# A one-core attention and expert layer: projections in another order, index scores and modulation sums beside a projection, suffix sums as fp32r products

## What is computed

```python
mod = silu(c) @ w_ada + b_ada            # six rows of 1024: shift1, scale1, gate1, shift2, scale2, gate2
h = rmsnorm(x, norm1_g) * (1 + scale1) + shift1
q_a,k_a,v_a, q_b,k_b,v_b, q_i,k_i,w_i, g_a,g_b = split(h @ w_in)   # four projections are 512 wide
# branch A, stick-breaking attention, 8 heads, strictly causal
z = q_a @ k_a.T * dh**-0.5
log_1m = where(before, log_sigmoid(-z), 0)
a = where(before, exp(log_sigmoid(z) + suffix_sum_of_later_keys(log_1m)), 0)
o_a = a @ v_a
# branch B: an indexer picks 128 keys for each query, then softmax attention with a position bias
score = sum_h w_i * relu(q_i @ k_i.T);  sel = top_k(score, 128)
o_b = softmax(rmsnorm(q_b) @ rmsnorm(k_b)[sel].T * dh**-0.5 + bias) @ v_b[sel]
x = x + gate1 * ((sigmoid(g_a)*(o_a @ w_o_a) + sigmoid(g_b)*(o_b @ w_o_b)) @ w_out)
# then a mixture of 16 experts, which the change leaves alone
```

## Time and profile before

| | |
|---|---|
| median of 3 runs | 805.81 us (804.68 to 807.87) |
| the profiled execution | 804.75 us, its span 802.8 us |
| PE busy | 747.3 us, 93% of the span |
| DVE busy | 615.5 us, 77% |
| ACT busy | 429.9 us, 54% |
| granted PE clock, mean | 0.988 |

### The profile page before, as it was taken

One profiled execution on the slowest core, in us unless ns is written; L12 is line 12 of the kernel. 1 busy time (PEld: TensorE's weight loads), 2 busy tenths in 40 slices (PEclk: granted clock), 3 DMA queues, 4 the chain that ended last, 5 costly groups with the idle time before them and its releaser, 6 DMA issues.

```text
span 802.8 us, 9975 instructions
## 1 busy us (share of the span) xinstructions
PE 747.3 (93%) x3617; PEld 569.3 (71%) x3619; DVE 615.5 (77%) x805; ACT 429.9 (54%) x516; POOL 109.2 (14%) x91
## 2 busy tenths in 40 slices
PE   3899999999999898999999988999999999999992
PEld 3777687776665555667888864788888887888782
DVE  5876886533999958653567657899999999999991
ACT  5433215357575443556423433776677777676760
POOL 4110000000010000002000011013233132413111
PEclk9999999999999999999999999999999999999997
DMA  9929996110130131105438246999999999999983
GB/s 268 353 79 383 386 362 229 52 53 1 53 106 1 55 103 53 53 7 196 138 116 298 111 176 209 415 399 373 385 387 386 387 387 386 387 385 381 372 289 56
DMA packets 87307, 184.93 MB, mean 230 GB/s; under 512 B 8112, under 2 KB 27672, under 8 KB 85216
## 3 DMA queue, kind: packets, MB, share of 16 engines
q1 hardware_dynamic: 79200, 156.29, 51.9%
q0 software_dynamic: 8064, 28.09, 12.2%
HBM read 171.74 MB, written 12.62 MB: 230 GB/s over the span
## 4 chain that ended last, share of the span: by engine, by line
PE 50%; DVE 28%; issue 7%; DMA 7%; ACT 5%; DVEq 1%; POOL 0%; SPq 0%; ACTq 0%; POOLq 0%
PE ps L666 13%; PE ps L668 12%; PE ps L667 12%; DVE w_lo L1963 8%; DMA raw<-in_w_gate 3%; DVE score L1783 3%; DVE m L1782 2%; DVE ys L2083 2%; ACT w_hi L1506 2%; DMA raw<-in_w_in 2%; DVE w_lo L1602 2%; PE ps L924 1%; DVE accm L1664 1%; DVE score L1769 1%; PE ps L940 1%
## 5 line engine op out<-in xcount | busy, mean ns | idle before, releaser
L1963 DVE TENSOR_TENSOR w_lo<-raw,w_hi 128x2048 fp32r<-128x2048 f32 x80 | 179.7, 2284 | 5.6 <-ACT w_hi L1506 5.6
L1506 ACT ACTIVATE w_hi<-raw 128x2048 fp32r<-128x2048 f32 x80 | 151.2, 1915 | 11.1 <-DMA raw<-in_w_gate 4.8
L666 PE MATMUL ps<-w_lo,hgT_hi 128*128 128x512 f32 x256 | 103.4, 404 | 4.6 <-DVE hgT_lo L2105 1.5
L666 PE MATMUL ps<-act_lo,w_hi 128*128 128x512 f32 x232 | 98.3, 424 | 5.1 <-DVE act_lo L1647 3.9
L667 PE MATMUL ps<-w_hi,hgT_lo 128*128 128x512 f32 x256 | 100.2, 391 | 0.0
L668 PE MATMUL ps<-w_hi,hgT_hi 128*128 128x512 f32 x256 | 100.0, 391 | 0.0
L668 PE MATMUL ps<-act_hi,w_hi 128*128 128x512 f32 x232 | 91.1, 393 | 0.0
L667 PE MATMUL ps<-act_hi,w_lo 128*128 128x512 f32 x232 | 91.0, 392 | 0.0
L1244 ACT ACTIVATE w_hi<-raw 128x2048 fp32r<-128x2048 f32 (+2 forms) x29 | 52.0, 1796 | 71.9 <-DMA raw<-in_w_in 48.8
L1602 DVE TENSOR_TENSOR w_lo<-raw,w_hi 128x2048 fp32r<-128x2048 f32 (+2 forms) x29 | 61.9, 2144 | 33.0 <-ACT w_hi L1244 32.8
L619 POOL DMA_INDIRECT out<-ys,slot_tok x15 | 48.9, 3257 | 159.9 <-DVE ys L2083 159.9
(11 more groups left out here) (283 smaller groups left out, 1361.8 us busy)
## 6 DMA issues: line engine op xcount, KB each, us to landing
raw<-in_w_down SPq DMA_DIRECT2D x32, 1024.0 KB, 15.7
raw<-in_w_gate SPq DMA_DIRECT2D x30, 1024.0 KB, 17.7
raw<-in_w_up SPq DMA_DIRECT2D x18, 1024.0 KB, 16.2
raw<-in_w_in SPq DMA_DIRECT2D x16, 1024.0 KB, 6.4
raw<-in_w_ada SPq DMA_DIRECT2D x16, 1024.0 KB, 7.2
raw_late<-in_w_up SPq DMA_DIRECT2D x14, 1024.0 KB, 18.2
raw<-in_w_ada SPq DMA_DIRECT2D x8, 512.0 KB, 6.7
raw_early<-in_w_ada SPq DMA_DIRECT2D x8, 512.0 KB, 6.5
```

Source lines behind the costliest of these rows:

```text
L666: pe.matmul(o, a[0], b[1], start=start, stop=False)
L1506: act.activation(e_hi[s_][:, :], e_raw[r][:, :], ACT.Copy).then_inc(e_top, 1)
L1963: dve.tensor_tensor(e_lo[s_][:, :], e_raw[r][:, :], e_hi[s_][:, :].bitcast(F32), ALU.subtract).then_inc(e_split, 1)
```

## The change

The order of the projections becomes qi, ka, qa, va, and that of the chunks qi, qi, 2 ada, ka, 3 ada, ka, 5 ada, qa, 6 ada, qa, va, va. The wait for a PSUM half is made bank by bank. DVE normalises q_b and k_b earlier: the squares after the first chunk of ka, the rest after the second. The transposes of q_b and k_b and the index products of query blocks 1 and 2 (11 tasks, `early_side`) are issued on PE between the half groups of the projection qa (a half group is six products), from the third half group on, in banks 4 to 7, which ka used; the first of them waits for ACT's copies of ka. The two modulation sums follow there as four products of 32 columns of ones each, into four quarters of one bank (`ada_sums`). DVE does the scores of blocks 1 and 2 and all 16 top-k rounds of block 1 before phase A. In phase A the mask is added to the logits right behind z (so line 1736 goes), line 1746's running sums go, ACT makes a float32r copy of the softplus tile (`soft_high`), DVE subtracts it (`soft_low`), and `suffix` multiplies both parts of the tile and of every later key block with the triangle and the matrix of -1 in fp32r. Two top-k rounds per step instead of three or four, none in phase B. Six gate products stand ahead of phase B's first logits.

```diff
+        add_in("qi", C_QI)
+        add_in("ka", C_KA)
         add_in("qa", C_QA)
-        add_in("ka", C_KA)
-        add_in("qi", C_QI)
         add_in("va", C_VA)
...
-        for ch, n in zip(chunks[N_EARLY:], (0, 0, 4, 4, 3, 5, 0, 0)):
+        for ch, n in zip(chunks[N_EARLY:], (0, 0, 2, 3, 5, 6, 0, 0)):
...
-        SEGS = [("misc", 1, None), ("qb", 0, False), ("qa", 1, True), ("ada1", 0, None),
-                ("ka", 1, True), ("ada2", 1, None), ("qi", 0, True), ("va", 1, False)]
+        SEGS = [("misc", 1, None), ("qb", 0, False), ("qi", 0, True), ("ka", 1, True), ("qa", 0, True), ("va", 1, False)]
...
+        N_TURN = 3
+        EARLY_SIDE = [("tr", n, 0) for n in range(N_TURN)] + [("idx", 1 + n // HP, n % HP) for n in range(2 * HP)]
+        SIDE_AT = 2
+        ADA_AT = SIDE_AT + len(EARLY_SIDE)
...
-        FILL_B = [4 * (len(STEPS) - 1) + 4 * (p + 1) for p in range(len(UNITS))]
+        FILL_T = 4 * (len(STEPS) - 1) + 6
+        FILL_B = [FILL_T + 4 * (p + 1) for p in range(len(UNITS))]
...
# PE, seg: bank by bank, and a call after every half group
+                        if ci == 0 and half_before(name):
+                            pe.wait_ge(evac[SEGS[seg_at[name]][1]], half_before(name) - 3 + m)
...
+                            if k == 1 and after:
+                                after(8 * ci + 2 * m)
...
+            def ada_sums(part):
+                pe.wait_ge(chunk_split, first[f"ada{part}"][-1] + 1)
+                pe.wait_ge(early_sb, len(EARLY_SIDE) - 1)
+                for j in range(4):
+                    last = pe.matmul(ps[5 + part][32 * j:32 * j + 32, :], ones[:, 0:32],
+                                     acc[part % 2][:, 512 * j:512 * j + 512], start=True, stop=True)
...
+            def early_side(n):
+                kind, a, hp = EARLY_SIDE[n]
+                b0 = 4 + 2 * (n % 2)
+                if n == 0:
+                    pe.wait_ge(qk_norm, 1)
+                    pe.wait_ge(evac[1], half_before("va"))
+                elif n >= 2:
+                    pe.wait_ge(early_sb, n - 1)
...
+            seg("qi", H)
+            pe.wait_ge(bias_sb, 2)
+            seg("ka", H)
+            seg("qa", H, None, beside_qa)
...
# PE, z and suffix
+                for r in range(2):
+                    last = pe.matmul(zt[m % 2][:, r, 0:P], identb[:, :], neg_ge[:, :], start=False, stop=False,
+                                     skip_group_check=True)
...
+                pe.wait_ge(sp_split, m + 1)
...
+                for j in range(i, NT):
+                    for part in (sp_lo, sp_hi):
+                        for r in range(2):
+                            last = pe.matmul(zt[m % 2][:, r, P * (j - i):S - P * i], neg_r[:, 1 if j > i else 0, :],
+                                             sp_tile(hp, j, part)[:, r, :], start=False,
+                                             stop=(j == NT - 1 and part is sp_hi), skip_group_check=True)
...
# ACT, after the copies of qb
             high(next(todo))
-            act.wait_ge(st_bias, 16)
+            act.wait_ge(qk_var, 1)
+            act.activation(st[:, :, :], st[:, :, :], ACT.Sqrt, bias=epsc[:, 0:1], scale=1.0 / DH).then_inc(qk_sd, 1)
             high(next(todo))
-            seg_copy("qa", qaT, SCALE)
+            seg_copy("qi", qiT)
             high(next(todo))
-            mod_rows(1)
             high(next(todo))
             seg_copy("ka", kaT)
+            for n in range(5):
+                early_side(n)
             high(next(todo))
...
# ACT, step m of phase A
                 gate_rows(FILL_A[m])
+                if m + 1 < len(STEPS):
+                    soft_high(m + 1)
                 weights(m)
...
# DVE
-            raw_chunks(first["va"][0] - N_EARLY - 1)
+            raw_chunks(first["ka"][0] - N_EARLY)
...
+            raw_chunks(first["ka"][1] - first["ka"][0])
             dve.wait_ge(qk_sd, 1)
...
-            raw_chunks(3)
+            raw_chunks(first["qa"][1] - first["ka"][1])
...
+            early_side(0)
+            early_side(1)
+            raw_chunks(1)
+            for q in range(2, 5):
+                early_side(q)
+            raw_chunks(1)
+            for q in range(5, 8):
+                early_side(q)
+            topk_rounds(TOPK // 8)
+            raw_chunks(1)
...
                 gate_splits(FILL_A[m])
-                topk_rounds(2)
-                sums(m)
-                topk_rounds(2 if m < 8 else 1)
+                topk_rounds(1)
+                if m + 1 < len(STEPS):
+                    soft_low(m + 1)
+                topk_rounds(1)
```

More of the change, by code:

```diff
@@ L697, in seg @@
                             last.then_inc(w_used, 1)
[L699 to L707, removed]
+                        if after:
+                            after(8 * ci + 2 * m + 1)
+            def ada_sums(part):
[4 more added lines that the diff above has]
+                                     acc[part % 2][:, 512 * j:512 * j + 512], start=True, stop=True)
+                last.then_inc(ada_ps, 1)
             pe.wait_ge(early_ok, 1)
@@ L857, in av_a, with side_task @@
                 last.then_inc(oa_ps, 1)
[L859 to L877, removed]
+            def side_task(hp):
+                if hp:
+                    pe.wait_ge(side_sb, hp)
+                for r in range(2):
+                    last = pe.matmul(sd[:, r, :], head(qiT, 2 * hp + r, S - P, S), kiT[DH * r:DH * r + DH, :],
+                                     start=True, stop=True, skip_group_check=True)
                 last.then_inc(side_ps, 1)
@@ L904, in _ @@
                     z(m + 1)
-                for t in side_a[m]:
-                    side_task(*t)
+                if 1 <= m <= N_SIDE:
+                    side_task(m - 1)
                 gates_to(FILL_A[m])
@@ L1294, in seg_copy, with mod_row, early_side @@
                     act.activation(dst[:, m, :], bank(name, m)[:, :], ACT.Copy, scale=scale).then_inc(evac[half], 1)
[L1296 to L1303, removed]
+            def mod_row(part):
+                act.wait_ge(ada_ps, part)
+                act.activation(modrow[part - 1][:, :], ps[5 + part][:, :], ACT.Copy).then_inc(ada_sb, 1)
+            def early_side(n):
+                kind, a, hp = EARLY_SIDE[n]
+                act.wait_ge(early_ps, n + 1)
+                b0 = 4 + 2 * (n % 2)
+                if kind == "idx":
+                    q = n - N_TURN
+                    if q >= 2:
+                        act.wait_ge(score_ok, 2 * (q - 1))
+                    act.activation(rel_early[q % 2][:, :, 0:P * (a + 1)], psum[:, b0:b0 + 2, 0:P * (a + 1)], ACT.Relu
+                                   ).then_inc(early_sb, 1)
+                elif a < 2:
+                    act.activation(qbT[:, 2 * a:2 * a + 2, :], psum[:, b0:b0 + 2, :], ACT.Copy, scale=SCALE
+                                   ).then_inc(early_sb, 1)
+                else:
+                    act.activation(kbT[:, :], ps[b0][:, :], ACT.Copy).then_inc(early_sb, 1)
             act.wait_ge(seg_ready, seg_done("misc", 0))
@@ L1363, in soft, with soft_high @@
                 act.activation(t, t, ACT.Ln, bias=1.0).then_inc(z_soft, 1)
+            def soft_high(m):
+                hp, i = STEPS[m]
+                act.wait_ge(sp_ready, m + 1)
+                act.activation(sp_tile(hp, i, sp_hi)[:, :, :], sp_tile(hp, i, sp_x)[:, :, :], ACT.Copy).then_inc(sp_high, 1)
             def weights(m):
@@ L1390, in _ @@
             soft(1)
+            soft_high(0)
             high(next(todo))
@@ L1773, in side_task, with early_side @@
                     rounds.extend((a, r) for r in range(TOPK // 8))
+            def early_side(q):
+                _, a, hp = EARLY_SIDE[N_TURN + q]
+                dve.wait_ge(early_sb, N_TURN + q + 1)
+                score_heads(a, hp, rel_early[q % 2])
+            def side_task(hp):
+                assert all(a != 1 for a, _ in rounds)
+                dve.wait_ge(side_sb, hp + 1)
+                score_heads(3, hp, rel)
             def topk_rounds(count):
@@ L1854, in _ @@
             dve.wait_ge(oa_ps, HP)
+            assert not rounds
             rows(0)
```

192 lines of the change are left out of this document (93 added, 99 removed).

## The result

The changed kernel takes 826.86 us (median of 4 runs, 825.09 to 831.66) against 806.72 for the kernel before in the same comparison (median of 4, 804.68 to 807.87): 1.0263 times as long, interval 1.0231 to 1.0295. Slower, as forecast, but by 20 us and not by 8; 826.9 lies outside 804 to 823. The profiled execution took 828.12 us, its span is 826.3.

What follows compares the result with a forecast made beforehand. PE was taken as the bounding engine, so only its idle time or removed work counts. Projection +18.2, phase A -8.0 and phase B -2 give +8.2 on the profiled 804.75: 813, as a median 814 us, range 804 to 823.

Steps and rivals of the forecast that it cites:

- Projection stage: Before phase A: PE waits 15.2 us for ka's copies at the first early task; phase A begins 18.2 us later.
- rival of dearer products: Quarter modulation sums run one after another (+4.7), narrow fp32r products cost 0.23 not 0.12 (some +3): 822 us; chance 0.17.
- Phase A: Removed mask and running-sum wait against a new softplus loop: 100.5 us instead of 108.55, -8.0.
- bounds of 92 to 105: Phase A's length: 92 if PE alone sets the pace, 105 if DVE's rounds and gate copies enter the loop.
- loop through `soft_high`: Phase A: weights(m) wait behind the next tile's float32r copy; 7.8 us per step for i = 0, 6.3 for i = 1.
- softplus that comes late behind the rounds: Phase A on DVE: without its cover, a softplus behind two rounds is late by up to a round, 1.5 us.
- Phase B: Gains of 4.9 and 1 us against +4 given back: sum -2, bounds 0 to -5.
- Given back: Phase B: gate and weight copies ahead of row sums, last vb product without cover: +4 us, from 0 to 7.
- The two gains named beside it: Phase B: block 3's rounds, idle time and lower clock go, -4.9; gate products fill idle time before the logits, -1.
- That PE alone sets phase A: Rival: PE's list hides the softplus loop in every step; phase A 92 us, total 805.5, no change; chance 0.13.
- ka's wait is short: Rival, first early task: second qa chunk lands earlier, giving 806 us, or 797 if before 116; chance 0.12.

Runs made afterwards that it cites:

- ka_copies_first: Changed kernel with ACT's copies of ka and first five early tasks ahead of the second qa chunk: 816.47 us, 1.0132 times the kernel before.
- two_ada_late_alone: Changed kernel with only the last two ada chunks moved behind the second chunk of qa: 823.4 us, 1.0223 times the kernel before.
- weights_first: Changed kernel with ACT's weights of step m ahead of the float32r copy of step m+1: 819.78 us, 1.0183 times the kernel before.
- gates_as_before: Changed kernel with the six gate products put back behind phase B's first logits: 815.85 us, 1.0144 times the kernel before.
- before_gates_moved: Kernel before with only the six gate products moved ahead of phase B's first logits: 814.31 us, 1.0112 times the kernel before.
- qa_copy_between_tasks: three_and_two_ada_late with ACT's copy of the second qa chunk ahead of the copies of index products 1 and 2: 797.36 us, 0.9885 times the kernel before.
- three_and_two_ada_late: Changed kernel with ka copies first, weights before float32r copy, gates as before, last two ada chunks behind qa's second chunk: 798.13 us, 0.9902 times the kernel before.
- after_again: The changed kernel run once more with no edit: 828.07 us, 1.0267 times the kernel before.

## Why the forecast was right about the direction and wrong about the size

The profiled execution is 23.5 us longer where 8.2 were forecast. Of the 15.3 us between, 7.6 are phase B, 3.7 the start, 2.8 phase A and 1.4 the projection stage. Phase B is the largest, but alone it would have left the forecast at 821.6, just inside its range; the others carry it out.

**Projection stage: right, step by step.** Forecast +18.2, measured +19.6. The first early task was to start 63.5 us into the stage (134.9 less 71.4) and started 63.8 in (138.87 less 75.1); behind it 53.7 were forecast and 54.8 measured. ka_copies_first and two_ada_late_alone show the cause: with the copies moved the wait goes, with the load 4.6 us earlier it shrinks by 4.5. The modulation sums, taken at 1.3 us each, took 1.07, nearer to 0.9 than to 3.67:

```profile
165.25 1.07 PE L711 MATMUL ps<-acc,ones 128*32 128x512 f32 x8
```

The Trainium skill, page TensorEngine Tiling (Array Packing), section Tiling Modes, has four tiles of 32 columns that work independently; this row agrees, as 3.67 / 4 is 0.92. The first half of the rival of dearer products falls with the 1.07.

**Phase A: right in its mechanism, short by a third of its gain.** Forecast -8.0, measured -5.2, inside the bounds of 92 to 105. The loop through `soft_high` sets the wide steps, as weights_first shows (-6.1 without it, with the window's PE busy time unchanged at 93). Steps i = 1 and 0 of the second pair and i = 3 of the third came out at the forecast's 6.3, 7.8 and 6.0 to within 0.1; in the third and fourth pair i = 1 takes 6.8. There the prediction had costed DVE at nothing, "under 90%", though it named a softplus that comes late behind the rounds as the possible price. DVE was busy for only 75.6 of the 103.3 us; it is the order of its list that tells, by the rows, as no run tests it alone: ACT's Ln is done at 255.5, and softplus starts 0.7 later, behind a round of block 3.

```profile
254.68 0.85 ACT L1401 ACTIVATE sp<-sp 128x768 f32<-128x768 f32 x1
```
```profile
255.49 0.68 DVE L1835 MATCH_REPLACE8 score<-m,score 128x512 f32<-128x512 f32 x1
256.20 0.96 DVE L1782 SCALAR_TENSOR_TENSOR sp<-ps,sp 128x768 f32<-128x768 f32 x1
```

z(15)'s chain takes 11.2 instead of 10.8, with 0.46 of wait for `soft_low`. These make half of the 2.8 us missed. The other half are smaller sizes: z(2) starts 2.4 us into the stage and not 1.9; i = 2 takes 6.6 in the third and fourth pair, where 6.4 were taken; and steps i = 3 and 2 of the second pair, where PE also does an index product of block 3 each, take 7.2 and 7.85, 0.65 more than forecast with the 2 us for these products. Without the loop, in weights_first, all these steps of i = 2 and 3 take the same, so the loop doesn't set them. The second half of the rival of dearer products falls: the suffix of i = 0 runs from 241.13 to 243.63, 2.5 us (forecast 2.55).

**Phase B: this step failed.** The prediction put it so: "Given back: the gate blocks now end ahead of a unit's row sums, so that ACT's gate copy and a weight copy of 1.9 stand before them every fourth unit, and the last product with vb has no gates to hide the transposed copies: I put +4, from 0 to 7." The place and the two waits were right; the term was mis-sized. The two gains named beside it came: 96.45 less these 4.9 and 1 is 90.5, and gates_as_before, which has the first but keeps the wait at the logits, measures 92.2. Against 90.5 the 102.0 us of the changed kernel are 11.5 given back, not 4, and above the upper bound of 7. They are 6.0 of the 6.9 us of waits for rows (0.9 at the first unit was there before too: 4.1 in two, of which the earlier trace rows shows 3.19), the 2.9 ahead of the last product, and the lower clock behind the two longest waits, by the windows shown 5.0 x 0.12 + 5.0 x 0.22 + 1.0 x 0.17 + 1.0 x 0.50 = 2.4: together 11.3.

Two links were missing in the sum. ACT doesn't only make the two copies ahead of the Exps, it first waits for the gate block to end, 3 to 7 us a time (`gate_b` waits 37.3 us in eight, 18.4 in the kernel before). And `obT_hi` stands behind the Exps, DVE waits for it with the row sums of the next unit queued behind (38.4 us in eight, 6.5 before). I had priced two copies; what counted was the chain of two engines that begins only when the block ends, against the 5 us that PE has until it needs the rows. That the gates' place alone makes this, gates_as_before and before_gates_moved show from both sides (-10 and +6.9). What each of the two links costs is read from the trace; no run separates them.

**The start.** 3.7 us of the profiled difference were no part of any step; they arise in the first 30 us, and I had no term for a span that starts late. Not all of them came with the lower clock of the last section: ACT's first `hfull` starts at 19.07 instead of 17.78, 1.3 us late, while the granted clock is still 1.00. Without the 3.7 the profiled execution lies 19.7 above that of before.

**The rivals.** That PE alone sets phase A is refuted (5.4 us of waits for weights); that ka's wait is short is refuted (14.12); dearer products are refuted by the rows above. 822 for that rival was the nearest number on record, and right for no reason it gave.

## What to carry to other kernels

When work is moved between two engines that hand each other small pieces, write down at which point of a unit each handed-over piece ends and what its consumer has queued behind it: gate products and their copies that moved from behind a unit's Exps to ahead of them cost 7 us in before_gates_moved with not one instruction added. A blocking wait is priced by what its engine does after it, on this engine and the next, and not by the copy itself: the copies of ka, the weights and the gates were all ready or nearly so, and late for a neighbour in the same list. Three reorderings of a few lines each turn this change from 20 us slower into 9 us faster, so a bad total does not condemn the parts.

## What was not expected of the hardware

The same instructions at the start of the program are granted different clocks in different executions. In the windows from 20 to 30 us the changed kernel had this:

```profile
20.00:22.00 2.00, 0.67 (x3) 1.00 1.04 352
22.00:24.00 2.00, 2.00 (x12) 0.55 1.04 347
24.00:26.00 2.00, 2.00 (x10) 0.50 1.12 359
```

and weights_first, whose program is the same up to phase A, this:

```profile
22.00:24.00 2.00, 2.00 (x16) 1.00 1.00 337
24.00:26.00 2.00, 1.67 (x10) 1.00 1.16 348
```

In both PE had stood 2.30 us for DVE's first `act_lo`, until 21.33 and until 20.46. Behind it one fell to 1.2 GHz for several us and the other stayed at 2.4. Of the twelve profiles, the start of the projection lies at 71.3 to 71.8 in four, and above 72.5 in eight. In phase B it is the same: behind a wait of 1.11 us ahead of the first logits, 274 to 284 us had 0.83 in qa_copy_between_tasks and 1.00 in three_and_two_ada_late. The Trainium skill, page TensorE: Matmul & The Clock Gate, section HAM oscillation — how this bites in real kernels, tells of idle gaps that bring the lower clock; the rows here agree that a wait of PE can cost twice. They also show that the same wait, of 2.30 or of 1.11 us, may or may not be followed by it. What decides it in one execution no run here was made to find, and it stays open. For a measurement, the medians of one kernel differ with no edit at all: by 1.2 us between after and after_again, and from 804.80 to 807.14 for the kernel before in its comparisons. So the length of the stage is to be compared.
